# A bidirectional retention and HGRN2 layer: the last head's key turn, two squares and a weight split on GpSimd, and where two evacuations stand

## The reference, cut to what matters

```python
shift, scale, gate = split(silu(c) @ w_ada + b_ada, 3)      # a row for context, a row for latents
h = rms_norm(x, norm_w) * (1 + scale) + shift
rq, rk, rv, rg, hq, hf_f, hf_b, hi, hg = split(h @ w_in, 9)   # 8 heads of 128 in each part
# group A: retention over chunks, both directions, states S
# group B: HGRN2, per channel decays b = cumsum(log f), both directions
#   s = exp(b_last) * s + (k * exp(b_last - b)).T @ v           <- the "keys" of this case: k * exp(b_last - b)
out = concat(norm(o_r) * silu(rg), norm(o_h) * silu(hg)) @ w_out
y = rms_norm(x + gate * out, final_norm_w)
```

## Time and profile before

| | us |
|---|---|
| median of 3 runs | 1402.96 (1402.95 to 1403.58) |
| the profiled execution's own time | 1402.7 |
| its span in the trace | 1400.9 |
| TensorE matmul busy | 1384.3 (99%) |
| VectorE busy | 1001.1 (71%) |
| ScalarE busy | 483.5 (35%) |
| GpSimd busy | 367.9 (26%) |

### The profile page before, as it was taken

The page is one execution under the profiler, slowest core; times in us unless marked ns, Lnnn a source line. Parts: engine busy times, 40 slices in busy tenths (PEclk is TensorE's granted clock), DMA queues, the critical chain, the costliest instruction groups (busy, mean ns, idle before and its releaser), DMA issues.

```text
span 1400.9 us, 24706 instructions
## 1 busy us (share of the span) xinstructions
PE 1384.3 (99%) x10042; PEld 1166.2 (83%) x10042; DVE 1001.1 (71%) x1330; ACT 483.5 (35%) x842; POOL 367.9 (26%) x292
## 2 busy tenths in 40 slices
PE   7999999999999999999999999999999999999997
PEld 5788898889888988898889888988898888888886
DVE  5655676667689888988888888877676768532345
ACT  4323243233333333342334333333333344221234
POOL 0000114311532153215321532153206225201220
PEclk9999999999999999999999999999999999999999
DMA  9995443435354535444444444433433357182235
GB/s 388 418 393 184 118 126 71 117 73 140 86 169 114 168 96 175 111 154 119 160 116 140 122 159 126 130 97 106 113 98 85 105 155 274 52 306 94 90 106 210
DMA packets 207735, 212.40 MB, mean 152 GB/s; under 512 B 144256, under 2 KB 156816, under 8 KB 202768
## 3 DMA queue, kind: packets, MB, share of 16 engines
q1 hardware_dynamic: 207600, 210.89, 47.8%
q10 hardware_dynamic: 32, 0.02, 0.0%
HBM read 182.27 MB, written 24.40 MB: 148 GB/s over the span
## 4 chain that ended last, share of the span: by engine, by line
PE 96%; DMA 2%; DVE 1%; SPq 0%; issue 0%; ACT 0%; DVEq 0%; ACTq 0%
PE ps L2130 10%; PE ps L2132 10%; PE ps L2131 10%; PE ps L1968 9%; PE ps L1970 8%; PE ps L1969 8%; PE ps L1944 8%; PE ps L2314 5%; PE ps L2316 5%; PE ps L2315 5%; DMA area<-in_w_mod 2%; PE ps L2147 2%; PE ps L1975 2%; PE ps L1976 2%; PE ps L1977 2%; PE ps L1934 2%
## 5 line engine op out<-in xcount | busy, mean ns | idle before, releaser
L1202 DVE TENSOR_TENSOR w_lo<-area,w_hi 128x1024 fp32r<-128x1024 f32 x143 | 190.4, 1331 | 208.0 <-ACT w_hi L730 207.9
L730 ACT ACTIVATE w_hi<-area 128x1024 fp32r<-128x1024 f32 x143 | 151.5, 1059 | 485.9 <-PE ps L2132 255.7
L2130 PE MATMUL ps<-w_hi,hT_hi 128*128 128x512 f32 x640 | 250.6, 392 | 0.0
L2131 PE MATMUL ps<-w_lo,hT_hi 128*128 128x512 f32 x640 | 249.2, 389 | 0.0
L2132 PE MATMUL ps<-w_hi,hT_lo 128*128 128x512 f32 x640 | 249.1, 389 | 0.0
L1968 PE MATMUL ps<-hT_hi,w_hi 128*128 128x512 f32 x512 | 204.9, 400 | 0.5 <-DVE hT_lo L1262 0.4
L1970 PE MATMUL ps<-hT_hi,w_lo 128*128 128x512 f32 x512 | 199.8, 390 | 0.0
L1969 PE MATMUL ps<-hT_lo,w_hi 128*128 128x512 f32 x512 | 199.8, 390 | 0.0
L2132 PEld LDWEIGHTS ps<-w_hi,hT_lo 128*128 128x128 f32 x640 | 120.2, 188 | 25.2
L2131 PEld LDWEIGHTS ps<-w_lo,hT_hi 128*128 128x128 f32 x640 | 120.2, 188 | 24.6
L2130 PEld LDWEIGHTS ps<-w_hi,hT_hi 128*128 128x128 f32 x640 | 120.2, 188 | 24.6
(11 more groups left out here) (282 smaller groups left out, 2429.1 us busy)
## 6 DMA issues: line engine op xcount, KB each, us to landing
area<-in_w_in SPq DMA_DIRECT2D x144, 512.0 KB, 4.4
area<-in_w_mod SPq DMA_DIRECT2D x26, 1024.0 KB, 12.1
area<-in_w_out SPq DMA_DIRECT2D x38, 512.0 KB, 3.7
gate_raw<-in_w_gate SPq DMA_DIRECT2D x32, 512.0 KB, 4.2
gate_raw<-in_w_mod SPq DMA_DIRECT2D x6, 1024.0 KB, 12.3
o_hi_scratch<-area SPq DMA_DIRECT2D x56, 80.0 KB, 2.4
o_lo_scratch<-area SPq DMA_DIRECT2D x56, 80.0 KB, 2.4
hT_hi<-o_hi_scratch SPq DMA_DIRECT2D x14, 320.0 KB, 7.1
```

The lines of the kernel that those rows point to most:

```text
L730: act.activation(split_weights(h, n)[0], raw[:, n % 3, :], ACT.Copy).then_inc(wt_hi.sem, 1)
L1202: v.tensor_tensor(lo, raw[:, n % 3, :], hi.bitcast(F32), ALU.subtract).then_inc(wt_lo.sem, 1)
L2130: mm(out, hT_hi[:, k, tile_cols(t)], w_hi[:, n % 2, w], start=k == 0, stop=False)
L2131: mm(out, hT_hi[:, k, tile_cols(t)], w_lo[:, n % 2, w], start=False, stop=False)
```

## The change

1. The last head turns its keys as the other heads do: `turn_keys(last)` on DVE behind `own_decay(last, 0)` and ahead of `split_w(1)`, and `move_keys(last)` on SP behind `load_w_out(2)`. PE's eight transposes and ACT's two copies go away, and `chunk_updates` keeps its place behind `first_block(0, kk, shared)`. On POOL, `key_factors(last)` moves ahead of `key_decay(last, 0)`.
2. While the last output block runs, `finish` of the block before is spread: tiles 0 and 1 behind chunk 1, tile 2 behind chunk 2, tile 3 behind chunk 3, tile 4 behind chunk 4.
3. In the front, the squares of slices 0 and 2 are made by POOL (`tensor_tensor`, 128x640), the other 14 by ACT.
4. `load(0, 0)` is issued behind modulation chunks 0 and 1. ACT's `split(0, 0)` moves behind the copy of `mod_row`, and its `w_lo` is made by POOL (128x1024) and no longer by DVE.

```diff
+POOL_SQUARES = (0, 2)
...
-            load(0, 0)
             chunks = {5: 1, 8: 2, 10: 3, 14: 4, 18: 5, 22: 6, 26: 7, 29: 8}
             for c_ in range(ADA_CHUNKS):
                 load_ada(c_)
+                if c_ == 1:
+                    load(0, 0)
...
             load_w_out(2)
+            move_keys(last)
             store_states(last, n_ret_f, n_ret_b, rst, r_state, r_state_stored)
...
-            for k in range(KT):
+            for k in [k for k in range(KT) if k not in POOL_SQUARES]:
...
-            split(0, 0)
             act.wait_ge(x_total.sem, x_total.at(SUMS - 1))
...
             act.activation(mod_row, ps[:, ada_bank(0), 0:ADA_TILE], ACT.Copy).then_inc(row_out.sem, 1)
+            split(0, 0)
...
-            keys(last)
...
             for j in range(1, len(DVE_SQUARES)):
-                dve.wait_ge(x_sq.sem, x_sq.at(DVE_SQUARES[j]))
+                if DVE_SQUARES[j] in POOL_SQUARES:
+                    dve.wait_ge(x_pool.sem, x_pool.at(len(POOL_SQUARES) - 1))
+                else:
+                    dve.wait_ge(x_sq.sem, squared(DVE_SQUARES[j]))
...
-            split(0, 0)
             dve.wait_ge(rstd_act.sem, rstd_act.at(0))
...
             own_decay(last, 0)
+            turn_keys(last)
             split_w(1)
...
+                    late = nb == OUT_BLOCKS - 1
                     if j == 1:
                         finish(nb - 1, 0, 2)
                     if j == 2:
-                        finish(nb - 1, 2, TILES)
+                        finish(nb - 1, 2, 3 if late else TILES)
+                    if late and j in (3, 4):
+                        finish(nb - 1, j, j + 1)
...
+            for k in POOL_SQUARES:
+                pool.wait_ge(x_landed[0].sem, x_landed[0].at(0))
+                g.tensor_tensor(x_squares[:, k % SQUARES, :], x_in[:, k, :], x_in[:, k, :], ALU.mult).then_inc(x_pool.sem, 1)
+            pool.wait_ge(wt_hi.sem, wt_hi.at(0, 1))
+            hi, lo = split_weights(0, 0)
+            g.tensor_tensor(lo, raw[:, 0, :], hi.bitcast(F32), ALU.subtract).then_inc(wt_lo.sem, 1)
...
+            key_factors(last)
             key_decay(last, 0)
-            key_factors(last)
...
-            def key_tokens(h):
...
+            def chunk_updates(h):
+
+                pe.wait_ge(k_moved.sem, k_moved.at(h))
                 pe.wait_ge(r_S.sem, r_S.at(h))
                 pe.wait_ge(r_state.sem, r_state.at(h))
...
-            pe.wait_ge(r_scaled.sem, r_scaled.at(last))
-            key_tokens(last)
             pe.wait_ge(h_sT.sem, h_sT.at(last, 3))
             for kk in range(WK):
                 first_block(0, kk, shared)
+            pe.wait_ge(r_scaled.sem, r_scaled.at(last))
             chunk_updates(last)
```

More of the change, by code:

```diff
@@ L282, in layer @@
         vec_landed = Signal("vec_landed", 16)
+        x_pool = Signal("x_pool")
         x_sq, x_sum, x_total = Signal("x_sq"), Signal("x_sum"), Signal("x_total")
@@ L325, in layer @@
         h_sq, h_rms, h_gated = Signal("h_sq"), Signal("h_rms", 2), Signal("h_gated")
-        last_keys, pe_hu, pe_level = Signal("last_keys", 2), Signal("pe_hu"), Signal("pe_level", PRODUCTS)
+        pe_hu, pe_level = Signal("pe_hu"), Signal("pe_level", PRODUCTS)
         pe_ho = Signal("pe_ho")
@@ L447, in gate_done, with squared @@
             return 2 * GATE_K * (c + 1)
+        def squared(k):
+            return x_sq.at(k) - sum(j <= k for j in POOL_SQUARES)
         CLASSES = ((1, slice(P, T)), (0, slice(0, P)))
@@ L858, in retention_norm @@
                 i.then_inc(r_scaled.sem, 1)
[L860 to L864, removed]
             def context_states(h):
@@ L1194, in _ @@
             pair = [x_squares[:, k % SQUARES, :] for k in LAST_SQUARES]
-            dve.wait_ge(x_sq.sem, x_sq.at(LAST_SQUARES[1]))
+            dve.wait_ge(x_sq.sem, squared(LAST_SQUARES[1]))
             v.tensor_tensor(pair[0], pair[0], pair[1], ALU.add).then_inc(x_sum.sem, 1)
@@ L2011, in _ @@
                 if j < len(PE_SQUARES):
-                    pe.wait_ge(x_sq.sem, x_sq.at(PE_SQUARES[j]))
+                    pe.wait_ge(x_sq.sem, squared(PE_SQUARES[j]))
                     squares = x_squares[:, PE_SQUARES[j] % SQUARES, :]
@@ L2198, in retention_columns @@
                 nc.tensor.transpose(ctx_columns(following), sT[:, 0:P], ident).then_inc(pe_columns.sem, 1)
-            def key_tokens(h):
-                pe.wait_ge(h_kl.sem, h_kl.at(h))
+            def chunk_updates(h):
+                pe.wait_ge(k_moved.sem, k_moved.at(h))
                 pe.wait_ge(r_S.sem, r_S.at(h))
                 pe.wait_ge(r_state.sem, r_state.at(h))
[L2205 to L2218, removed]
                 for i, t in enumerate((0, 1, 2, 3)):
```

## The result

The changed kernel takes 1406.57 us (median of 8 runs, 1406.20 to 1408.83) against 1402.89 us for the kernel before in the same rounds (median of 8). The ratio is 1.003 with a 95% interval of 1.0021 to 1.0039: it is slower, by 3.7 us. The profiled execution took 1406.57 us, of which the span is 1404.8, that is 3.9 more than the span of before.

A forecast was written before the change was run, and what follows sets the result against it. PE, busy 99% of the span, was taken as the bound, with transfers a floor at 64.33 us in the front. 1.5 + 2.16 - 0.6 - 0.5 + 1.3 = +3.9 us gave 1406.8 us, range 1404.0 to 1409.2.

The forecast's parts named there:

- Front, the split: Front: POOL's w_lo holds DVE's L1238, so first_group starts about 29.6 instead of 27.93; +1.5 us, bounds 0 and +2.2.
- Load order: Front: chunks 0 and 1 land 1.25 us sooner, chunk 2's landing stays at 26.88; zero.
- Clock: Front and tail: longer PE gaps lower the granted clock; 1.3 us lost in all, bounds 0 and 1.7 for each place.
- Tail, POOL's order: Tail: key_factors moved ahead holds DVE, L1329 ends at 1158.17 and delays PE's first output matmul; +2.16 us, bounds 0 and 2.8.
- Tail, the keys: Tail: PE loses eight transposes, 0.88 us, partly lost waiting for DVE's split at first_block(2, 0); -0.6 us, bounds -0.97 and -0.3.
- The spread: Last block: DVE's split ends before PE asks, so PE's wait goes; -0.5 us, bounds -0.5 and 0.
- The squares: Front: two squares on POOL, 1.4 us each, priced at nothing; bounds -0.4 and +0.8 us.
- POOL yielding: Rival, front and tail: POOL runs only where DVE is idle, nothing is held; 1401.9 us, chance 0.06.
- the free front: Rival, front: POOL falls beside small or PSUM-reading instructions, so its hold costs nothing; +1.1, 1404.1 us, chance 0.10.
- a part that does not bite: Rival: the squares or the order on POOL move differently than expected; about 1404 us, no chance of its own.
- late keys: Rival, tail: slow key write and reads make PE wait in chunk_updates; 1412 us at 10 us each, chance 0.05.
- No fall of the clock: Rival, front and tail: the same holds, 2.6 us, without a lower clock; 1405.6 us, chance 0.20.

The follow-up runs named there:

- the split on DVE: The changed kernel with the first w_lo made on DVE, ahead of slice 0's norm, in place of POOL: 1405.73 us, ratio to before 1.0022.
- the front alone: The change's front edits (squares, load order, split) with the tail of the kernel before: 1405.53 us, ratio 1.0019.
- the same with idle matmuls: The front alone plus idle(11) ahead of chunk 2 and idle(6) behind it: 1404.40 us, ratio to before 1.0010.
- the profile with idle matmuls: The changed kernel plus idle matmuls around chunk 2 and nine ahead of first_block(0, 0): 1405.07 us, ratio to before 1.0015.
- the tail alone: The front of the kernel before with all three tail edits (key turn, POOL's order, spread): 1405.35 us, ratio 1.0016.
- the old order: The tail alone with key_decay(last, 0) ahead of key_factors(last) on POOL again: 1402.82 us, ratio to before 1.0000.
- the fastest version: The old order with turn_keys behind retention_chain and load_w_out(3) and (4) issued ahead of move_keys: 1401.81 us, ratio to before 0.9992.
- with the stall filled: The tail alone plus nine 128x128 matmuls ahead of first_block(0, 0): 1403.80 us, ratio to before 1.0007.

## Why the prediction was right, and where it was not

The forecast was 1406.8, a sum of +3.9; measured were 1406.57 and +3.7 at the medians, +3.9 in the spans. Step by step:

- **Front, the split: right.** Forecast +1.5, `first_group` at 29.6. It started at 29.70 (+1.77); with the clock held up the front costs 1.6 us. POOL came at 24.09 (forecast 24.0) and held DVE 2.0 us (2.31 less 0.29), until it ended at 26.82 where I had put 26.7. The Trainium skill's GPSIMD Engine Reference, section 4.1, gave +1.8 by its factor of two, which is as near.
- **Load order: right on the transfers, wrong as "zero".** Chunk 2 landed at its old time. But chunks 0 and 1 came sooner, PE stood idle 2.6 to 2.9 us ahead of chunk 2 instead of 1.64, and the clock fell, with POOL's hold or without it (the split on DVE). I had this in the clock's term and not in the load's.
- **Clock: the size right (1.3 forecast, 1.5 measured), in part by luck, and the split of it partly open.** I had sized one fall by the 0.57 of the earlier trace rows, and that fall cost its own run at most 0.15 us (27.93 against 27.78); the 1.3 was a choice inside wide bounds. The front's share is 1.1 (the front alone against the same with idle matmuls). The tail's is 1.55 when the tail stands alone, and most of its executions have it. In the changed kernel both together are 1.5 (1406.57 less 1405.07), and the profiled execution shows no fall in the tail: it and the profile with idle matmuls are already 1.42 us apart at the first output matmul (1161.08 and 1159.66). This is also why front alone and tail alone, +2.7 and +2.5, do not add up to the +3.7 of the whole, while with idle matmuls +1.6 and +1.0 come near the whole's +2.2. The two runs of the changed kernel at 1408.6 and 1408.8 have a mean clock of 0.994, where the others have 0.995 or 0.996, as if the tail's fall came only there. Why it comes less often behind the changed front, no run here shows.
- **Tail, POOL's order: right.** +2.16 forecast, +2.15 in the tail alone, +2.41 in the changed kernel, 2.5 us back with the old order. There DVE's split ahead of `differences` started 2.78 us later than before (1153.27 against 1150.49), 0.26 more than PE's own lateness, and DVE's queue hands that on.
- **Tail, the keys: the sum right, the reason incomplete.** -0.6 forecast and -0.60 measured, with the wait for DVE's split in the place I had given. But I costed the turn on DVE at nothing because of a split that follows it, and did not ask when `key_factors` ends. The turn is free only with the order on POOL that makes PE's stall: with that undone it blocks DVE for 2.86 us and PE for 0.84, and the gain of the transposes is lost.
- **The spread: right**, -0.5 forecast, no pause left in the profile, -0.6 at the medians when it stands alone, which is inside that run's interval.
- **The squares: right**, priced at nothing; -0.4 at the medians, which was my lower bound and can't be told from nothing. They took 1.23 us each and not 1.4.

Of the rivals, POOL yielding falls by L1241 and L1477, the free front by 29.70, a part that does not bite by both places being held, and late keys by the profile of the changed kernel, where `chunk_updates` does not wait. "No fall of the clock" was 1405.6; the run that prevents the fall has 1405.07, so the price of that rival was half a microsecond high, less than such a median can settle.

## What to carry to other kernels

Before work goes to POOL, look at what DVE runs in the microseconds in which POOL will: a long POOL instruction holds a 0.3 us link of DVE's chain for its whole length, and it pays to cut it in pieces, or to leave it on DVE, if that chain leads to PE (though here neither brought the front back to what it was). A transfer that comes sooner can cost time: ask what the longer gap behind it does to TensorE's clock, and fill a gap that can't be closed with matmuls of no account. And price an edit again without its neighbours: the key turn was free only with an order on POOL that made a stall elsewhere, and the fastest version, 1.06 us under before and not yet clear of no change, needed the turn, POOL's order and SP's loads moved together.

## What the runs showed of the hardware

- DVE and POOL alternate whole instructions. A DVE instruction of 0.29 us took 2.31 beside one POOL instruction of 128x1024, and 0.42 beside eight of 128x128. The eight lasted 4.88 us together, the one 2.56 (2.73 in the changed kernel).
- Whether the clock falls behind the same stall of 2.2 us is not the same from execution to execution: seven of eleven executions of the tail alone were some 1.5 us longer at a lower mean clock, four were not, and with the stall filled none was. One profile does not show it; the mean granted clock of all executions does.
